# GpSimd makes the token combinations of both feed-forward beginnings piece by piece, and two of their low parts

## The reference, cut to what matters

```python
D_FF = 2816

def swiglu(h, w_in, w_out):
    gu = h @ w_in
    gate, up = jnp.split(gu, 2, axis=-1)
    return (jax.nn.silu(gate) * up) @ w_out

for i in range(DEPTH):          # DEPTH = 2
    ...
    h = rmsnorm(x, norm_ffn[i]) * (1 + sc2) + sh2
    x = x + g2 * swiglu(h, ffn_w_in[i], ffn_w_out[i])
```

## Time and profile before

| what | value |
| --- | --- |
| median of 3 runs | 2672.32 us (2672.22 to 2672.35) |
| the profiled execution, its own time | 2670.46 us |
| its span, first to last instruction | 2668.7 us |
| PE busy | 2588.7 us (97%) |
| DVE busy | 1885.1 us (71%) |
| ACT busy | 1022.1 us (38%) |
| POOL (GpSimd) busy | 331.5 us (12%) |
| step 1 of the first feed-forward | 440.02 to 477.57 us |
| step 1 of the second feed-forward | 1550.33 to 1587.83 us |

### The profile page before, as it was taken

One profiled execution on the slowest core, in us unless ns is written; L12 is line 12 of the kernel. 1 busy time (PEld: TensorE's weight loads), 2 busy tenths in 40 slices (PEclk: granted clock), 3 DMA queues, 4 the chain that ended last, 5 costly groups with the idle time before them and its releaser, 6 DMA issues. The chain is left out here.

```text
span 2668.7 us, 35605 instructions
## 1 busy us (share of the span) xinstructions
PE 2588.7 (97%) x12898; PEld 2063.0 (77%) x12898; DVE 1885.1 (71%) x3089; ACT 1022.1 (38%) x1833; POOL 331.5 (12%) x455
## 2 busy tenths in 40 slices
PE   6999899999999999999999989999999999999998
PEld 5666587788888888777776768888888887888987
DVE  6888857877777777745656788777777777433565
ACT  5444726333333333445445453333333333111243
POOL 2011003000000000201110210000000027971000
PEclk9999999999999999999999999999999999999999
DMA  6333221111111111223232111111111122113122
GB/s 238 116 129 135 92 90 52 56 51 55 54 52 48 55 55 44 105 68 97 94 105 88 48 32 56 51 51 55 51 55 47 55 63 92 48 48 58 32 95 79
DMA packets 170955, 193.10 MB, mean 72 GB/s; under 512 B 8000, under 2 KB 136224, under 8 KB 170432
## 3 DMA queue, kind: packets, MB, share of 16 engines
q1 hardware_dynamic: 158256, 147.45, 17.1%
q0 software_dynamic: 12592, 44.21, 5.4%
HBM read 177.86 MB, written 12.58 MB: 71 GB/s over the span
## 5 line engine op out<-in xcount | busy, mean ns | idle before, releaser
L2534 DVE SCALAR_TENSOR_TENSOR xT<-psum,mod,xT 128x1024 f32<-128x1024 f32 x352 | 446.2, 1279 | 146.1 <-PE psum L1506 146.0
L1506 PE MATMUL psum<-hT_high,w_low 128*128 128x512 f32 x1344 | 360.5, 390 | 6.7 <-DVE xT L2534 6.6
L1506 PEld LDWEIGHTS psum<-hT_high,w_low 128*128 128x128 f32 x1344 | 251.6, 188 | 62.7 <-DVE xT L2534 11.0
L1964 ACT ACTIVATE w_high<-wpair 128x512 fp32r<-128x512 f32 x294 | 184.8, 632 | 244.3 <-DMA wpair<-in_ffn_w_in_dram 132.8
L1192 PE MATMUL psum<-hT_high,w_low 128*128 128x512 f32 x864 | 244.2, 395 | 2.3 <-DVE arena L3047 2.1
L1506 PE MATMUL psum<-h_low,w_low 128*128 128x512 f32 x672 | 207.6, 390 | 2.2 <-DVE h_low L2529 2.2
L1275 PE MATMUL psum<-hT_high,w_low 128*128 128x512 f32 x480 | 202.1, 421 | 0.9 <-DVE h_low_mix L2472 0.7
L1474 PE MATMUL psum<-hT_high,w_high 128*128 128x512 f32 x504 | 196.6, 390 | 0.0
L1475 PE MATMUL psum<-h_low,w_high 128*128 128x512 f32 x504 | 196.6, 390 | 0.0
L1476 PE MATMUL psum<-hT_high,w_low 128*128 128x512 f32 x504 | 196.4, 390 | 0.0
L1192 PEld LDWEIGHTS psum<-hT_high,w_low 128*128 128x128 f32 x864 | 162.6, 190 | 39.1 <-issue 2.5
(11 more groups left out here) (380 smaller groups left out, 5156.0 us busy)
## 6 DMA issues: line engine op xcount, KB each, us to landing
wpair<-in_ffn_w_in_dram SPq DMA_DIRECT2D x176, 256.0 KB, 2.9
wpair<-in_ffn_w_out_dram SPq DMA_DIRECT2D x88, 256.0 KB, 2.7
wpair<-in_ada_tiles_dram POOLq DMA_DIRECT2D x20, 1024.0 KB, 5.3
wpair<-in_ada_tiles_dram POOLq DMA_DIRECT2D x32, 512.0 KB, 3.6
wpair<-in_w_in_dram SPq DMA_DIRECT2D x24, 512.0 KB, 3.8
wpair<-in_b_tiles_dram SPq DMA_DIRECT2D x18, 512.0 KB, 3.3
arena<-in_ada_tiles_dram SPq DMA_DIRECT2D x8, 1024.0 KB, 16.3
out_dram<-xT SPq DMA_DIRECT2D x16, 512.0 KB, 3.3
```

The costliest lines, as they stand in the source:

```text
L1506: mm = nc.tensor.matmul(dst[:, HALF * t:HALF * t + HALF], w, src[:, t, :], start=n == 0, stop=n == 2)
L1964: nc.scalar.activation(part_high[name], part_raw[name], ACT.Copy).then_inc(part_high_ready, 1)
L2534: nc.vector.scalar_tensor_tensor(xT[:, m, :], acc[m % 2] if src is None else src, mod[:, l, 40 + m:41 + m], xT[:, m, :], ALU.mult, ALU.add ...
```

## The change

GpSimd makes all four token combinations, in sixteen pieces of 128x512, in the order T1, T3, T2, T4, and then the low parts of T1 and T4, each in one instruction of 128x2048. DVE keeps the low parts of T3 and T2, and loses T3, T4 and the low parts of T1 and T4: four instructions of 128x2048 in each feed-forward. T3's pieces wait for ScalarE's shift of chunk 4 + k and for DVE's `half_low` of chunk k, T2's for that of chunk 4 + k. DVE's low part of T2 waits for all of T4 too. ScalarE makes the high parts in the order T3, T1, T2, T4. PE's P5 and P4 now wait for GpSimd (`front_ready`) and not for DVE. PE's order is unchanged, as are the DMAs.

```diff
+TOKEN_TURN = ("T1", "T3", "T2", "T4")
+HIGH_TOKENS = ("T3", "T1", "T2", "T4")
...
+def token_number(f, name):
+
+    return 16 * f + 4 * TOKEN_TURN.index(name) + 4
...
@@ -980,15 +987,20 @@
-                for k in range(4):
-                    pool.wait_ge(shifted, shift_number(2 * f + 1, k, 1))
-                    nc.gpsimd.tensor_tensor(token_raw["T1"][:, k, :], token_raw["T3"][:, k, :], token_raw["B11"][:, k, :],
-                                            ALU.subtract).then_inc(token_made, 1)
-                for n in range(2):
-                    rows = slice(2 * n, 2 * n + 2)
-                    pool.wait_ge(token_made, 8 * f + n + 5)
-                    nc.gpsimd.tensor_tensor(token_raw["T2"][:, rows, :], token_raw["T2"][:, rows, :], token_raw["T1"][:, rows, :],
-                                            ALU.subtract).then_inc(token_made, 1)
+                for n, (name, x, y, read, shift) in enumerate((("T1", "T3", "B11", None, 0), ("T3", "T2", "T3", 0, 4),
+                                                               ("T2", "T2", "T1", 4, None), ("T4", "T4", "T2", None, None))):
+                    for k in range(4):
+                        if n:
+                            pool.wait_ge(token_made, 16 * f + 4 * n + k - 3)
+                        if shift is not None:
+                            pool.wait_ge(shifted, shift_number(2 * f + 1, shift + k, 1))
+                        if read is not None:
+                            pool.wait_ge(h_ready, h_number(2 * f + 1, read + k))
+                        nc.gpsimd.tensor_tensor(token_raw[name][:, k, :], token_raw[x][:, k, :], token_raw[y][:, k, :],
+                                                ALU.subtract).then_inc(token_made, 1)
+                for name in ("T1", "T4"):
+                    pool.wait_ge(token_high_ready, 4 * f + HIGH_TOKENS.index(name) + 1)
+                    nc.gpsimd.tensor_tensor(token_low[name], token_raw[name], as_f32(token_high[name]), ALU.subtract).then_inc(front_ready, 1)
...
@@ -1513,18 +1525,18 @@
-                    pe.wait_ge(token_split, 4 * f + 1)
+                    pe.wait_ge(token_split, 2 * f + 1)
                     with_token(1, "P7", "S3", "e", "T3")
                     down(0, 0, [4], True)
                     pe.wait_ge(product_kept, kept_number(f, 1, "P1"))
-                    pe.wait_ge(token_split, 4 * f + 2)
+                    pe.wait_ge(token_split, 2 * f + 2)
                     with_token(1, "P6", "S2", "a", "T2", False)
                     down(0, 0, [5], True)
                     pe.wait_ge(product_kept, kept_number(f, 1, "P6"))
-                    pe.wait_ge(token_split, 4 * f + 3)
+                    pe.wait_ge(front_ready, (KC + 2) * l + KC + 1)
                     with_token(1, "P5", "S1", "a", "T1", False)
                     down(0, 0, [6], True)
-                    pe.wait_ge(token_split, 4 * f + 4)
+                    pe.wait_ge(front_ready, (KC + 2) * l + KC + 2)
                     with_token(1, "P4", "A22", "e", "T4", False)
...
@@ -1990,16 +2002,16 @@
-                    token(1, "T3")
+                    token("T1")
                     keep(1, "P3", gate_half[:, 1, :], bank["c"])
                     high(1, "S1")
-                    token(3, "T2")
+                    token("T2")
...
-                    token(4, "T4")
+                    token("T4")
...
                 hidden_high(0, 0, first=True)
-                token(0, "T1")
+                token("T3")
                 second_step()
...
@@ -2508,14 +2520,11 @@
-                def token(n, name, x, y, ks):
-
-                    dve.wait_ge(token_made, 8 * f + n + 4)
-                    nc.vector.tensor_tensor(token_raw[name][:, ks], token_raw[x][:, ks], token_raw[y][:, ks], ALU.subtract).then_inc(token_made, 1)
-
-                def token_lows(n, name):
-
-                    dve.wait_ge(token_high_ready, 4 * f + n + 1)
+                def token_lows(name, after):
+
+                    dve.wait_ge(token_high_ready, 4 * f + HIGH_TOKENS.index(name) + 1)
+                    if after:
+                        dve.wait_ge(token_made, token_number(f, after))
...
@@ -2546,23 +2555,19 @@
-                    token(0, "T3", "T2", "T3", slice(0, 4))
+                    token_lows("T3", None)
                     add_down(0, 0)
                     add_down(0, 1)
-                    token_lows(1, "T3")
                     add_down(0, 2)
                     down_lows(0, 1)
                     low(1, "S2")
                     combine(1, "S1", first=True)
-                    token(3, "T4", "T4", "T2", slice(0, 4))
-                    token_lows(2, "T2")
+                    token_lows("T2", "T4")
                     dve.wait_ge(product_kept, kept_number(f, 1, "P1"))
                     add(1, "X0", gate_half[:, 0, :], gate_half[:, 0, :], bank["b"], "P2")
                     low(1, "S1")
-                    token_lows(0, "T1")
                     add_down(0, 3)
                     low(1, "A22")
-                    token_lows(3, "T4")
                     add_down(0, 4)
```

More of the change, by code:

```diff
@@ L1451, in first_step @@
                             if half == 0:
-                                pe.wait_ge(front_ready, KC * l + k + 1)
+                                pe.wait_ge(front_ready, (KC + 2) * l + k + 1)
                             else:
@@ L1964, in high, with token @@
                     nc.scalar.activation(part_high[name], part_raw[name], ACT.Copy).then_inc(part_high_ready, 1)
-                def token(n, name):
-                    act.wait_ge(token_made, 8 * f + n + 4)
+                def token(name):
+                    act.wait_ge(token_made, token_number(f, name))
                     nc.scalar.activation(token_high[name], token_raw[name], ACT.Copy).then_inc(token_high_ready, 1)
```

## The result

The changed kernel takes 2682.55 us in the median of 5 runs (2679.12 to 2687.23), the kernel before 2672.22 us beside it (2667.31 to 2672.35, 5 runs). The ratio is 1.0044, with a 95% interval of 1.003 to 1.0057: slower by 10.3 us, where 14.7 were forecast. The time lies inside the range of 2677 to 2695 us, but 0.5 us under 2683, where the forecast's own bounds begin. The profiled execution of the changed kernel took 2679.12 us, 8.7 more than that of before.

What follows compares the result with a forecast made beforehand. DVE was taken to bound the feed-forward stretch where PE waits; GpSimd's holds outweigh the relief. Per feed-forward 6.5 us plus 1 us of clock, twice, +15 us on 2672.3: 2687 us, range 2677 to 2695 (own bounds 2683 to 2695).

Steps and rivals of the forecast that it cites:

- third rival: DVE's back-to-back instructions keep GpSimd out; T2 and T4 end late, downs +4.2 us, twice, 2681 us; chance 0.09.
- DVE's instructions are held by GpSimd's, one and one: Where both queues are full, DVE waits for the rest of GpSimd's instruction, GpSimd for all of DVE's; 1.19 us each.
- The price of a piece: GpSimd's sixteen pieces take some 1.8 us each, T4 ending at 456.4; DVE's two-SBUF-operand instructions wait 1.19 us each.
- P2 +6.5 us, the new first wait: Step 1, first feed-forward: the low part of A12 ends at 449.2, and PE's P2 waits for it, +6.5 us.
- T1's low part: On GpSimd, 4.75 us, until 463.3; `down_lows` waits 0.75 us, T2's low part ends at 469.8, P6 +6.6 us.
- `combine` behind T4's low part: Step 2's S3 on DVE, asked at 474.0, waits 4.2 us; PE's down 0 of step 2 comes +6.5 us.
- The clock: PE's longer waits may bring low-clock stretches, 2.9 us on P2 and P3 or 0.6 on P6; 1 us taken per feed-forward.
- The first three: Rivals: hold misses DVE's queue, 2662 us (0.06); 0.45 us lost per instruction, 2667 (0.06); GpSimd kept out, 2681 (0.09).
- The fourth: Rival: the clock falls in every long wait, 6.5 + 2.9 + 1.8 us, twice, 2695 us; chance 0.06.

Runs made afterwards that it cites:

- memsets: Changed kernel with GpSimd's pieces of T3, T2 and T4 replaced by three memsets each of 128x512, which read nothing: 2674.09 us.
- copies: Changed kernel with GpSimd's subtractions for T3, T2 and T4 replaced by copies of the first operand, in the same 12 pieces: 2671.13 us.
- halves: Changed kernel with GpSimd's combinations T3, T2 and T4 in halves of 128x1024 instead of quarters of 128x512: 2689.84 us.

## Why the prediction was right, and where it was off

The direction and the mechanism were right, the size was 4.4 us too high. The time is inside the range, but the range reached below 2683 us only to take in the third rival, whose mechanism did not occur; so that the number fell inside is in part luck.

- **DVE's instructions are held by GpSimd's, one and one.** Right, and shown from three sides: gone with memsets, smaller with copies, larger with halves. The rule of the Trainium skill, page "SBUF — State Buffer", section "SBUF: two separate sides", says exclusive lock and whole instruction, and of a DVE instruction with two SBUF inputs that it counts only against a GpSimd operation that reads SBUF. The runs agree with all of it: 0.68 us beside memsets, 0.91 to 1.10 beside copies, 1.57 to 1.77 beside subtractions. No run here shows how the two come to alternate.
- **The price of a piece.** A little too high, and this is the term that was mis-sized. I took 1.8 us between pieces and 1.19 us of hold; the pieces came at 1.71, and the holds were 0.88 to 1.09 us (1.57 - 0.69, 1.77 - 0.68). Sixteen pieces ended at 455.13, not at 456.4 plus the 0.9 us by which this execution began them later (427.82 against 426.91 in the earlier trace rows), 2.2 us sooner. Half of that is a slip of the text: twelve pieces of 1.8 us from the end of T1's, 426.91 + 6.92 = 433.83, end at 455.4 and not at 456.4.
- **P2 +6.5 us, the new first wait.** It came at +6.1, 5.2 without those 0.9. The wait itself is 2.04 us and not the 5 to 7 of the text, since PE came to P1 1.2 us late and P1 had then waited 1.71 us for the low part of A11: DVE ended that at 443.75. I had walked DVE's queue through `half_low` and A11 and not asked who waits for them. P2 waits for DVE either way, so it starts no later for that.
- **T1's low part.** 4.6 us of work where I took 4.75; its row shows 6.57 because it was asked while DVE's T3 low ran, the hold in the other direction. `down_lows`, which was to wait 0.75 us behind it, did not: at 462.71 it came right behind the end at 462.36. T2's low part ran at 467.11, P6 came at +5.2 net, forecast +6.6. P4 at 479.37 against 473.49 is +5.0 net, as forecast, but by chance: with down 5's wait of 1.54 us gone it would have been +3.7, and P6's matmuls at the lower clock level (470.44 above) took some 1.4 us more.
- **`combine` behind T4's low part.** 4.70 us, so a hold of 4.0 for the 4.2 forecast, but asked 1.4 us sooner than in the walk, since all before it was sooner. The first down came +4.9 and +4.7 us, forecast +6.5. Twice 1.7 us is most of the 4.4 us by which the total was too high.
- **What the change is, by its parts.** The text had the low parts and the combinations in one walk. The runs take them apart: combinations +5.3, low parts +2.9, both +4.9 us. The second does not add to the first.
- **The clock.** I allowed 2 us in all. The two distances sum to +9.6 us and the medians to +10.3, so no more than 0.7 us is left for it, less than the two can be told apart. Low stretches came, but where PE would have waited anyway: P2 of the first feed-forward ran at half speed for 3 us (449.75 above) and took 1.7 us longer, and P3 still had to wait for DVE; in the second, P2 ran at full speed, and the distances differ by 0.2 us. The text had priced such a stretch at up to 2.9 us. The low stretch behind 491 us in the first feed-forward has no fellow at that place in the second.
- **The rivals.** The first three are excluded by the rows above: no relief reached the downs, each instruction lost twice 0.45 us and not once, and GpSimd was not kept out (1.71 us a piece). The third would have given 2681 us, nearer to the measured time than the forecast, by another way: a right-looking number isn't its mechanism. The fourth, a fall of the clock in every long wait at 2695 us, is excluded by the time; the clock did fall on P6 in both feed-forwards and on P2 in the first, not on P2 in the second.

## What to carry to other kernels

Work taken from VectorE by GpSimd is no relief where VectorE's queue holds instructions with two SBUF operands back to back: here a subtraction of 128x512 saved VectorE about 0.55 us and cost it 0.9 to 1.1. Put such work beside VectorE's PSUM-reading instructions, and cut it into short pieces where VectorE would run into its start (1 us gained here, and nothing where VectorE met its end). Work that VectorE did while it waited for another engine, as T4's combination here, is no relief at all. When walking a queue, name the waiter of every instruction in it, not of the ones that the change is about.

## What the runs showed that was not expected

- GpSimd's three memsets of 128x512, 0.53 us each, cost VectorE nothing, and its one-operand copy, 0.62 us alone, costs it 0.2 to 0.4 us. It is the reading and the length of the instruction that count, not GpSimd's being busy.
- The same low part of T1 on GpSimd held one VectorE instruction for 0.2 us when begun at 451.61, and another for 4.2 us when begun at 453.63: a few microseconds in the two queues decide whether it is free.
- A low stretch of the clock can cost nothing: with pieces of double size P1 ran at the lower level and took 2.5 us longer, all of it time in which P2 would have waited for VectorE.
